# Decoder layer in split float32: the order of the products inside a weight slot pair, bank by bank or product by product

## The chip, the cores and the metric

One core of a Trainium2 chip runs one launch of the kernel. The metric is device time in microseconds (us). Before the change the median of three runs is 2539.82 us, the lowest 2538.85 and the highest 2540.03.

## The reference, cut to what matters

The reference is one step (one layer) of a hybrid decoder on 256 prompt tokens and 8 x 4 sample tokens, 288 in all, with width 2048:

```python
x = x + 0.5 * _swiglu(_rmsnorm(x, g_ffn1), w1_gate, w1_up, w1_down)   # 2048 -> 5504 -> 2048
h = _rmsnorm(x, g_mix)
proj = h @ w_in                                                        # 2048 -> 7192
...        # forgetting attention on 8 heads, mLSTM on 8 heads, causal convolution, gates
x = x + y @ w_out                                                      # 2048 -> 2048
x = x + 0.5 * _swiglu(_rmsnorm(x, g_ffn2), w2_gate, w2_up, w2_down)
# _swiglu(x, g, u, d) = (silu(x @ g) * (x @ u)) @ d
```

All is float32, and the answer has to be near float32 accuracy. The time lies in the eight big products with a weight matrix (gate, up and down twice, w_in, w_out); all weights are read from HBM once.

## The kernel before, in words

**Split operands.** A float32 matrix is cut into two parts that TensorE multiplies in its faster rounded type: `hi`, the value rounded, and `lo`, what is left. A product w * x is the sum of three: w_hi * x_hi, w_hi * x_lo and w_lo * x_hi. The activations stand transposed, one tile of 128 rows by T = 288 tokens for each of the 16 (or 24, or 19) blocks of the contraction, and they are the moving operand. A 128 x 128 block of the weights is the stationary operand, loaded anew for each matmul.

**Slots, turns and pairs.** The weights come in pieces of 128 x 1024 float32 (512 KB), one per block of the contraction, into `w_raw`, which has four slots. SyncE issues the transfers. ScalarE rounds a slot into `w_hi` (L544), VectorE subtracts to make `w_lo` (L766). Four slots are a turn. TensorE works through a turn in two pairs of slots; it waits for both `w_lo` of the pair, and its last matmul of the pair raises `w_used`, which lets ScalarE overwrite the pair.

**Groups and banks.** A group is an output of up to 8 blocks of 128 columns, accumulated in the 8 banks of PSUM over 4 turns (contraction 2048), 6 turns (3072) or 5 turns (19 blocks, so that the last pair holds one slot). The groups in order, with their number: `gu0a` 6, `down0a` 2, `gu0b` 4, `gu0c` 1 (with 6 banks), `down0b` 2 (19 blocks), then the mixer `in_a` 3, `in_m` 4 and `out` 2, then `gu1a` to `down1b` as in the first SwiGLU. In a gate and up group (`gu...`) the even banks hold gate blocks, the odd ones up blocks.

**Order inside a pair.** The function `turn_products` goes bank by bank: for a bank, for each slot of the pair, the three products (L1257, L1258, L1259), so 6 matmuls in a row write one bank before the next bank has its 6. That makes 48 matmuls a pair.

**Handing over the banks.** There is one set of 8 banks, so a group writes where the one before it wrote. In the last pair of a group each bank is closed after its 6 matmuls (`bank_done`, or `w_used` for the last bank), and the bank is read while TensorE closes the others. In a gate and up group ScalarE takes SiLU of an even bank (L598) and VectorE multiplies with the odd bank (L839); a multiply frees its two banks, and the last multiply frees all that are left (banks 4 to 7 in `gu0c` and `gu1c`). In a down group VectorE adds each bank to the residual `X` (L867), in `in_a` and `in_m` it copies it out (L918, L1112 and L1113, L1117). Each raises `banks_free`. In its first pair the next group waits for `banks_free` ahead of its first matmul into each bank.

**Order of the other engines.** Each has one list written by hand, in loops. VectorE prepares the first two slots of the next group (L766) and then empties the banks.

Of the kernel before, what the change touches and what calls it, by code (L numbers as in the profile page):

```python
# [37 lines left out]
P = 128  # L38
# [6 lines left out]
T = TP + SM  # L45
# [14 lines left out]
SLOTS = 4  # L60
NBANK = 8
# [32 lines left out]
def build(nc, A, O):  # L94
# [48 lines left out]
    w_hi, w_lo = t_("w_hi", [P, SLOTS, UW], F32R), t_("w_lo", [P, SLOTS, UW], F32R)  # L143
# [6 lines left out]
    ps = ctx.enter_context(nc.psum_tensor("ps", [P, NBANK, 512], F32))  # L150
# [103 lines left out]
    w_hi_ready, w_lo_ready, w_used = sem("w_hi_ready"), sem("w_lo_ready"), sem("w_used")  # L254
    bank_done, banks_free = sem("bank_done"), sem("banks_free")
# [986 lines left out]
    def _(pe):  # L1242
        mm, tr = nc.tensor.matmul, nc.tensor.transpose

        def turn_products(g, turn0, gi, kt, x_hi, x_lo, first, last, x_ready):

            for pair in range(2):
                slots = [s for s in (2 * pair, 2 * pair + 1) if not (last and 0 < g.real % SLOTS <= s)]
                pe.wait_ge(w_lo_ready, (turn0 + kt) * SLOTS + (2 * pair + 2))
                pe.wait_ge(x_ready[0], kt * SLOTS + (x_ready[1] + slots[-1] + 1))  # L1250
                for b, c in enumerate(g.tiles):
                    if first and pair == 0:
                        pe.wait_ge(banks_free, gi * NBANK + (b + 1))
                    out = ps[:, b, 0:T]
                    for s in slots:
                        hi, lo, k = w_hi[:, s, c:c + P], w_lo[:, s, c:c + P], kt * SLOTS + s
                        mm(out, hi, x_hi[:, k, :], start=first and pair == 0 and s == slots[0], stop=False)  # L1257
                        mm(out, hi, x_lo[:, k, :], start=False, stop=False)  # L1258
                        ins = mm(out, lo, x_hi[:, k, :], start=False, stop=last and pair == 1 and s == slots[-1])  # L1259
                    if b == len(g.tiles) - 1:  # L1260
                        ins.then_inc(w_used, 1)
                    elif last and pair == 1:
                        ins.then_inc(bank_done, 1 if b < len(g.tiles) - 2 else NBANK + 1 - len(g.tiles))

        def group_products(g, i, x_hi, x_lo, x_ready):

# [56 lines left out]
        for t in range(KD):  # L1323
            if t >= 4:
                pe.wait_ge(sem("xT_copied"), t - 3)
            for r, n in TT:
                ins = tr(ps[:, 1 + t % 4, r * P:r * P + n], x_rows[0:n, r, t * P:(t + 1) * P], ident[0:n, 0:n])
# [18 lines left out]
        for k in range(KD):  # L1346
# [3 lines left out]
            ins = mm(gates, w_gates_lo[:, k, :], xm_hi[:, k, :], start=False, stop=k == KD - 1)  # L1350
# [3 lines left out]
        for t, n in TT:  # L1354
            ins = tr(ps[0:n, 3, t * 3 * H:(t + 1) * 3 * H], gates_row[:, t * P:t * P + n], ident[0:3 * H, 0:3 * H])
# [94 lines left out]
        for h in range(H):  # L1450
            ins = mm(bhq(ps[0:SM, 7, 0:256])[:, :, h, :], ka[:, h, TP:T], qa[:, h, TP:T], start=True, stop=True)
# [12 lines left out]
        for g2 in range(2):  # L1464
# [6 lines left out]
            ins = mm(o2, spread[:, r], mask4_q[:, :], **add)  # L1471
        ins.then_inc(sem("sample_logits"), 1)
        for g2 in range(2):
# [3 lines left out]
            ins = tr(ps[0:SM, 1, g2 * P:(g2 + 1) * P], Ps[:, g2, 2 * P:T], ident[:, :])  # L1477
# [6 lines left out]
        for p in range(NB * NPG):  # L1484
            pe.wait_ge(sem(f"v_loaded{p % VRING}"), 16 * (p // VRING + 1))
            pe.wait_ge(sem("pz_ready"), p + 1)
            for h in range(H):
                ins = mm(ps[0:SM, 2 + h // 4, h % 4 * HD:(h % 4 + 1) * HD], pz[:, p % 4, h * SM:(h + 1) * SM],  # L1488
                         v_page[p % VRING][:, h * HD:(h + 1) * HD], **add)
            ins.then_inc(sem("sample_pv"), 1)  # L1490
        for h in range(H):
            pe.wait_ge(sem("out_rows_ready"), 1 + h // 4)
            ins = tr(ps[:, 1, h * SM:(h + 1) * SM], out_rows[:, h * HD:(h + 1) * HD], ident[0:SM, 0:SM])
# [19 lines left out]
        for j in range(2 * H):  # L1513
            ins = tr(ps[:, 5, j * 24:(j + 1) * 24], conv_rows[0:24, j * P:(j + 1) * P], ident[0:24, 0:24])
# [8 lines left out]
        for b in range(2):  # L1523
            for j in range(4):
                ins = mm(ps[:, 6 + b, j * 96:(j + 1) * 96], sel[:, 4 * b + j, :].bitcast(F32), s_rows[:, :, :], start=True, stop=True)
# [136 lines left out]
```

## Time and profile before

| | |
|---|---|
| median of 3 runs | 2539.82 us |
| span of the profiled execution, first to last instruction | 2540.0 us |
| TensorE busy, matmuls | 2423.9 us, 95%, 17636 records |
| TensorE weight loads | 2348.2 us, 92% |
| VectorE busy | 1197.0 us, 47% |
| ScalarE busy | 905.7 us, 36% |
| mean granted TensorE clock | 0.971 |
| DMA | 151 GB/s mean, 46.8% of the queues' time on the main one |

The profile page gives no other time for that execution than its span. It lies 0.2 us above the median of the runs, so terms read from the trace can be added to the median as they are. Matmuls overlap one another: one that lasts 0.29 us starts 0.13 us after the one before it, so a pace is read from starts, not from durations. A time such as 105.92 is counted from the start of the span.

### The profile page before, as it was taken

The page shows a single profiled execution, that of the slowest core. Times are in us where ns is not written, and L with a number is a line of the kernel's source. Part 1 is how long each engine was busy: PE and PEld are TensorE (multiplying, and loading weights), DVE is VectorE, ACT ScalarE, POOL GpSimd, SP SyncE. Part 2 cuts the span into 40 slices and gives each one's busy share as a digit, 9 for nine tenths or more (in the row PEclk, how much of TensorE's full clock was granted, in tenths as well). Part 3 has the DMA queues.
Part 4 walks back from the last instruction along what each step waited for, and adds up shares of the span by engine and source line. Part 5 has one row for each costly group of instructions (what it writes and reads, how often), then busy time and mean ns, then how long its engine had stood idle before and what let it go on. Part 6 is the DMA issues. An engine that isn't in the chain of part 4 may idle for free.

```text
span 2540.0 us, 47708 instructions
## 1 busy us (share of the span) xinstructions
PE 2423.9 (95%) x17636; PEld 2348.2 (92%) x17636; DVE 1197.0 (47%) x1664; ACT 905.7 (36%) x1139; POOL 83.7 (3%) x96
## 2 busy tenths in 40 slices
PE   5999999999999989898899897989999999999997
PEld 4999999999999989778899875979999999999997
DVE  5444544344454464543347665454444444444543
ACT  3444433333343433321234323344444333333432
POOL 1000000000000000000000241000000000000000
PEclk9999999999999999989999887989999999999998
DMA  3555555555555535434255441435555444555553
GB/s 108 166 165 165 165 166 165 164 166 165 166 167 166 166 117 165 159 102 158 89 165 165 130 115 39 166 108 158 165 165 166 164 164 162 167 165 162 169 172 127
DMA packets 172981, 383.79 MB, mean 151 GB/s; under 512 B 18629, under 2 KB 44333, under 8 KB 172285
## 3 DMA queue, kind: packets, MB, share of 16 engines
q1 hardware_dynamic: 170144, 374.94, 46.8%
q0 software_dynamic: 2432, 5.57, 0.7%
q10 hardware_dynamic: 336, 2.36, 0.2%
q8 instruction: 44, 0.72, 0.1%
q14 instruction: 25, 0.20, 0.0%
HBM read 373.09 MB, written 9.70 MB: 151 GB/s over the span
## 4 chain that ended last, share of the span: by engine, by line
PE 91%; DVE 6%; ACT 1%; issue 1%; DMA 1%; POOL 0%; SPq 0%; ACTq 0%; DVEq 0%; POOLq 0%
PE ps L1259 27%; PE ps L1257 27%; PE ps L1258 27%; PE ps L1431 1%; PE ps L1283 1%; PE ps L1488 1%; DVE xt L811 1%; PE ps L1594 1%; DMA w_raw<-in_w_up 1%; PE ps L1585 1%; DVE w_lo L766 1%; PE ps L1292 1%; PE ps L1299 1%; PE ps L1418 1%; DVE x_lo L801 0%
## 5 line engine op out<-in xcount | busy, mean ns | idle before, releaser
L766 DVE TENSOR_TENSOR w_lo<-w_raw,w_hi 128x1024 fp32r<-128x1024 f32 x674 | 795.6, 1222 | 1109.8 <-ACT w_hi L544 1109.8
L544 ACT CAST w_hi<-w_raw 128x1024 fp32r<-128x1024 f32 x674 | 673.9, 1047 | 1294.5 <-PE ps L1259 1279.9
L1257 PE MATMUL ps<-x_hi,w_hi 128*128 128x288 f32 (+1 forms) x2752 | 817.6, 297 | 19.2 <-DVE x_lo L801 14.7
L1259 PE MATMUL ps<-x_hi,w_lo 128*128 128x288 f32 (+1 forms) x2752 | 819.3, 298 | 0.0
L1258 PE MATMUL ps<-x_lo,w_hi 128*128 128x288 f32 (+1 forms) x2752 | 805.9, 293 | 0.0
L1257 PEld LDWEIGHTS ps<-x_hi,w_hi 128*128 128x128 f32 x2752 | 520.4, 189 | 20.2 <-issue 20.2
L1258 PEld LDWEIGHTS ps<-x_lo,w_hi 128*128 128x128 f32 x2752 | 528.4, 192 | 0.0
L1259 PEld LDWEIGHTS ps<-x_hi,w_lo 128*128 128x128 f32 x2752 | 518.8, 189 | 0.0
L1257 PE MATMUL ps<-hid_hi,w_hi 128*128 (+1 forms) x1376 | 407.6, 296 | 1.5 <-DVE X L867 1.5
L1258 PE MATMUL ps<-hid_lo,w_hi 128*128 (+1 forms) x1376 | 406.2, 295 | 0.0
L1259 PE MATMUL ps<-hid_hi,w_lo 128*128 (+1 forms) x1376 | 405.0, 294 | 0.0
L1257 PE MATMUL ps<-xm_hi,w_hi 128*128 128x288 f32 (+1 forms) x896 | 267.5, 299 | 12.2 <-DVE xm_lo L801 7.1
L1259 PE MATMUL ps<-xm_hi,w_lo 128*128 128x288 f32 (+1 forms) x896 | 267.6, 299 | 0.0
L1258 PE MATMUL ps<-xm_lo,w_hi 128*128 128x288 f32 (+1 forms) x896 | 263.4, 294 | 0.0
L1257 PEld LDWEIGHTS ps<-hid_hi,w_hi 128*128 128x128 f32 x1376 | 258.1, 188 | 1.9 <-DVE X L867 1.9
L1259 PEld LDWEIGHTS ps<-hid_hi,w_lo 128*128 128x128 f32 x1376 | 259.4, 188 | 0.0
L1258 PEld LDWEIGHTS ps<-hid_lo,w_hi 128*128 128x128 f32 x1376 | 258.4, 188 | 0.0
L1257 PEld LDWEIGHTS ps<-xm_hi,w_hi 128*128 128x128 f32 x896 | 170.4, 190 | 13.0 <-issue 13.0
L1258 PEld LDWEIGHTS ps<-xm_lo,w_hi 128*128 128x128 f32 x896 | 173.1, 193 | 0.0
L1259 PEld LDWEIGHTS ps<-xm_hi,w_lo 128*128 128x128 f32 x896 | 169.8, 190 | 0.0
L1257 PE MATMUL ps<-y_hi,w_hi 128*128 128x288 f32 (+1 forms) x256 | 76.8, 300 | 1.4 <-DVE y_lo L801 1.4
L1259 PE MATMUL ps<-y_hi,w_lo 128*128 128x288 f32 (+1 forms) x256 | 76.8, 300 | 0.0
(405 smaller groups left out, 1595.7 us busy)
## 6 DMA issues: line engine op xcount, KB each, us to landing
w_raw<-in_w_down SPq DMA_DIRECT2D x178, 512.0 KB
w_raw<-in_w_gate SPq DMA_DIRECT2D x320, 256.0 KB
w_raw<-in_w_up SPq DMA_DIRECT2D x320, 256.0 KB
w_raw<-in_w_in SPq DMA_DIRECT2D x112, 512.0 KB
w_raw<-in_w_out SPq DMA_DIRECT2D x32, 512.0 KB
page<-in_cache_k SPq DMA_DIRECT2D x16, 512.0 KB, 3.4
w_raw<-in_w_gate SPq DMA_DIRECT2D x32, 192.0 KB
w_raw<-in_w_up SPq DMA_DIRECT2D x32, 192.0 KB
```

The source lines that it names most:

```text
L544: nc.scalar.copy(w_hi[:, slot, :], w_raw[:, slot, :]).then_inc(w_hi_ready, 1)
L766: nc.vector.tensor_tensor(w_lo[:, slot, :], w_raw[:, slot, :], w_hi[:, slot, :].bitcast(F32), ALU.subtract).then_inc(w_lo_ready, 1)
L811: nc.vector.scalar_tensor_tensor(xt[:, t % 2, :], X[:, t, :], vecs[:, gain + t:gain + t + 1], rs[:, 1, :], ALU.mult, ALU.mult).then_inc(se ...
L1257: mm(out, hi, x_hi[:, k, :], start=first and pair == 0 and s == slots[0], stop=False)
L1258: mm(out, hi, x_lo[:, k, :], start=False, stop=False)
L1259: ins = mm(out, lo, x_hi[:, k, :], start=False, stop=last and pair == 1 and s == slots[-1])
L1283: mm(ps[:, bank, 0:T], ones[:, :], sq_ring[i % 4], start=stop_start[0], stop=stop_start[1]).then_inc(sem("sum_done"), 1)
L1292: mm(out, sel[:, h, :], parts[0], start=start, stop=False)
L1299: mm(ps[0:H, bank + j // H, 0:T], one_hot[:, j % H, :], sq_ring[(i0 + j) % 4], start=j % H == 0, stop=j % H == H - 1).then_inc(sem("sum_do ...
L1418: ins = tr(ps[:, 5 + 2 * half, i * P:(i + 1) * P], page[:, p % 3, c:c + HD], ident[:, :])
L1431: ins = mm(ps[r:r + SM, 6, col:col + P], qz[:, b % 2, h * SM:(h + 1) * SM], kpT[:, p % 2, h * HD:(h + 1) * HD], start=b < 4 and c == 0 and ...
L1488: ins = mm(ps[0:SM, 2 + h // 4, h % 4 * HD:(h % 4 + 1) * HD], pz[:, p % 4, h * SM:(h + 1) * SM], v_page[p % VRING][:, h * HD:(h + 1) * HD] ...
```

## The change: products outside, banks inside

In every pair but the last of a group, the loops are turned round: for each slot of the pair, for each of the three products, all eight banks (six in `gu0c` and `gu1c`). So eight matmuls in a row share the moving operand and go to eight banks. The last pair of a group keeps the old order, since the banks are closed there one after another. Number, shapes and operands of the matmuls are the same. `w_used` is raised by the last matmul of a pair, as before. The wait for each bank in a group's first pair stands ahead of the first matmul into that bank, as before. No other engine's list changes. All three products now stand on one line (L1257).

```diff
-                for b, c in enumerate(g.tiles):
-                    if first and pair == 0:
-                        pe.wait_ge(banks_free, gi * NBANK + (b + 1))
-                    out = ps[:, b, 0:T]
+                n, ending = len(g.tiles), last and pair == 1
+
+                def product(out, s, c, part, start, stop):
+
+                    k = kt * SLOTS + s
+                    w, x = ((w_hi, x_hi), (w_hi, x_lo), (w_lo, x_hi))[part]
+                    return mm(out, w[:, s, c:c + P], x[:, k, :], start=start, stop=stop)
+
+                if ending:
+                    for b, c in enumerate(g.tiles):
+                        for s in slots:
+                            for part in range(3):
+                                ins = product(ps[:, b, 0:T], s, c, part, False, s == slots[-1] and part == 2)
+                        if b == n - 1:
+                            ins.then_inc(w_used, 1)
+                        else:
+                            ins.then_inc(bank_done, 1 if b < n - 2 else NBANK + 1 - n)
+                else:
                     for s in slots:
-                        hi, lo, k = w_hi[:, s, c:c + P], w_lo[:, s, c:c + P], kt * SLOTS + s
-                        mm(out, hi, x_hi[:, k, :], start=first and pair == 0 and s == slots[0], stop=False)
-                        mm(out, hi, x_lo[:, k, :], start=False, stop=False)
-                        ins = mm(out, lo, x_hi[:, k, :], start=False, stop=last and pair == 1 and s == slots[-1])
-                    if b == len(g.tiles) - 1:
-                        ins.then_inc(w_used, 1)
-                    elif last and pair == 1:
-                        ins.then_inc(bank_done, 1 if b < len(g.tiles) - 2 else NBANK + 1 - len(g.tiles))
+                        for part in range(3):
+                            for b, c in enumerate(g.tiles):
+                                opening = first and pair == 0 and s == slots[0] and part == 0
+                                if opening:
+                                    pe.wait_ge(banks_free, gi * NBANK + (b + 1))
+                                ins = product(ps[:, b, 0:T], s, c, part, opening, False)
+                    ins.then_inc(w_used, 1)
```

The opening pair of a group, on TensorE, before (`x_hi` and `x_lo` are the moving operand; `REGISTER_ALU` sets the number that the next wait compares with):

```order
L1253 ISA [waits xn_ready,w_lo_ready]
L1257 MATMUL ps<-x_hi,w_hi 128x288 [waits banks_free]
L1258 MATMUL ps<-x_lo,w_hi 128x288
L1259 MATMUL ps<-x_hi,w_lo 128x288
L1257 MATMUL ps<-x_hi,w_hi 128x288
L1258 MATMUL ps<-x_lo,w_hi 128x288
L1259 MATMUL ps<-x_hi,w_lo 128x288
L1253 REGISTER_ALU
L1257 MATMUL ps<-x_hi,w_hi 128x288 [waits banks_free]
```

The same pair on TensorE in the changed kernel, from the seventh bank's wait on; six such matmuls with a wait, one per bank, stand ahead of it:

```order
L1257 MATMUL ps<-x_hi,w_hi 128x288 [waits banks_free]
L1274 REGISTER_ALU
L1257 MATMUL ps<-x_hi,w_hi 128x288 [waits banks_free]
L1257 MATMUL ps<-x_lo,w_hi 128x288 x8
L1257 MATMUL ps<-x_hi,w_lo 128x288 x8
L1257 MATMUL ps<-x_hi,w_hi 128x288 x8
L1257 MATMUL ps<-x_lo,w_hi 128x288 x8
L1257 MATMUL ps<-x_hi,w_lo 128x288 x8
L1249 REGISTER_ALU
```

The eight waits for a bank stood ahead of the 1st, 7th, 13th ... 43rd matmul of the group; they now stand ahead of the 1st, 2nd, 3rd ... 8th.

Inside the loop over the middle turns, one pair on TensorE before, its first matmuls:

```order
L1250 ISA [waits w_lo_ready]
L1257 ISA [waits xn_ready]
L1257 MATMUL ps<-x_hi,w_hi 128x288
L1258 REGISTER_ALU
L1258 MATMUL ps<-x_lo,w_hi 128x288
L1259 MATMUL ps<-x_hi,w_lo 128x288
```

The same pair in the changed kernel, whole:

```order
L1250 ISA [waits w_lo_ready]
L1257 ISA [waits xn_ready]
L1257 MATMUL ps<-x_hi,w_hi 128x288 x8
L1257 REGISTER_ALU
L1257 MATMUL ps<-x_lo,w_hi 128x288 x8
L1257 MATMUL ps<-x_hi,w_lo 128x288 x8
L1257 ISA
L1257 MATMUL ps<-x_hi,w_hi 128x288 x8
L1257 REGISTER_ALU
L1257 MATMUL ps<-x_lo,w_hi 128x288 x8
L1257 MATMUL ps<-x_hi,w_lo 128x288 x8
```

The waits and the register instructions of such a pair are the same, in front of the same products; what moved is only the order of its 48 matmuls.

## Rows read from the trace of the kernel before

**Rows 1.** The page: busy times; TensorE's busy tenths and granted clock in 40 slices.
```profile
PE 2423.9 (95%) x17636; PEld 2348.2 (92%) x17636; DVE 1197.0 (47%) x1664; ACT 905.7 (36%) x1139; POOL 83.7 (3%) x96
PE   5999999999999989898899897989999999999997
PEclk9999999999999999989999887989999999999998
```
**Rows 2.** The page's groups: line, operation, tiles, count | busy us, mean ns | idle before.
```profile
L1257 PE MATMUL ps<-x_hi,w_hi 128*128 128x288 f32 (+1 forms) x2752 | 817.6, 297 | 19.2 <-DVE x_lo L801 14.7
L1257 PE MATMUL ps<-hid_hi,w_hi 128*128 (+1 forms) x1376 | 407.6, 296 | 1.5 <-DVE X L867 1.5
L1257 PE MATMUL ps<-xm_hi,w_hi 128*128 128x288 f32 (+1 forms) x896 | 267.5, 299 | 12.2 <-DVE xm_lo L801 7.1
L1257 PE MATMUL ps<-y_hi,w_hi 128*128 128x288 f32 (+1 forms) x256 | 76.8, 300 | 1.4 <-DVE y_lo L801 1.4
```
**Rows 3.** Timeline, TensorE: first matmul of four groups. Start us, duration us, what.
```profile
105.92 0.30 PE L1257 MATMUL ps<-x_hi,w_hi 128*128 128x288 f32 x1
...
156.70 0.30 PE L1257 MATMUL ps<-x_hi,w_hi 128*128 128x288 f32 x1
...
359.79 0.30 PE L1257 MATMUL ps<-hid_hi,w_hi 128*128 128x288 f32 x1
...
436.58 0.30 PE L1257 MATMUL ps<-hid_hi,w_hi 128*128 128x288 f32 x1
```
**Rows 4.** Timeline, TensorE: the matmuls from one bank to the next.
```profile
106.46 0.29 PE L1258 MATMUL ps<-x_lo,w_hi 128*128 128x288 f32 x1
106.59 0.30 PE L1259 MATMUL ps<-x_hi,w_lo 128*128 128x288 f32 x1
106.73 0.29 PE L1257 MATMUL ps<-x_hi,w_hi 128*128 128x288 f32 x1
```
**Rows 5.** Timeline, TensorE: the gates, 24 weight columns; 14 rows between these left out.
```profile
1052.79 0.29 PE L1349 MATMUL ps<-xm_lo,w_gates_hi 128*24 128x288 f32 x1
...
1054.77 0.29 PE L1349 MATMUL ps<-xm_lo,w_gates_hi 128*24 128x288 f32 x1
```
**Rows 6.** Timeline, TensorE, at a granted clock of 0.50; 5 rows between left out.
```profile
67.09 0.44 PE L1257 MATMUL ps<-x_hi,w_hi 128*128 x1
...
68.53 0.44 PE L1257 MATMUL ps<-x_hi,w_hi 128*128 x1
```
**Rows 7.** Timeline, VectorE, where the down group at 816.22 follows another.
```profile
813.44 2.36 DVE L766 TENSOR_TENSOR w_lo<-w_raw,w_hi 128x1024 fp32r<-128x1024 f32 x2 [4.04 <-ACT w_hi L544]
815.71 3.00 DVE L867 SCALAR_TENSOR_TENSOR X<-ps,X 128x288 f32<-128x288 f32 x8
```
**Rows 8.** Timeline, TensorE, the same place.
```profile
815.18 0.29 PE L1259 MATMUL ps<-hid_hi,w_lo 128*128 128x288 f32 x1
816.22 0.40 PE L1257 MATMUL ps<-hid_hi,w_hi 128*128 128x288 f32 x1 [0.74 <-DVE X L867]
816.45 0.29 PE L1258 MATMUL ps<-hid_lo,w_hi 128*128 128x288 f32 x1
816.58 0.29 PE L1259 MATMUL ps<-hid_hi,w_lo 128*128 128x288 f32 x1
```
**Rows 9.** Timeline: first matmul after `gu0c`, and the last multiply of `gu0c`.
```profile
754.56 0.30 PE L1257 MATMUL ps<-hid_hi,w_hi 128*128 128x288 f32 x1
...
754.86 0.45 DVE L839 TENSOR_TENSOR prod<-silu,ps 128x288 f32<-128x288 f32 x1 [0.63 <-PE ps L1259]
```
**Rows 10.** Timeline: last reading of the banks at three group starts, and the third start.
```profile
106.20 0.46 DVE L839 TENSOR_TENSOR prod<-silu,ps 128x288 f32<-128x288 f32 x1 [1.13 <-PE ps L1259]
436.78 0.46 DVE L867 SCALAR_TENSOR_TENSOR X<-ps,X 128x288 f32<-128x288 f32 x1 [0.34 <-PE ps L1259]
...
1278.02 0.30 PE L1257 MATMUL ps<-xm_hi,w_hi 128*128 128x288 f32 x1
...
1278.57 0.18 DVE L1113 COPY ext<-ps 128x32 f32<-128x32 f32 x1
```
**Rows 11.** Windows: us, busy us (count) by engine, granted clock, DMA share, GB/s.
```profile
62.90:66.20 3.30, 0.87 (x7) 0.64 (x5) 2.59 (x3) 3.30 (x4) 0.00 (x0) 1.00 0.07 7
66.20:69.60 3.40, 3.38 (x14) 3.39 (x15) 2.04 (x2) 1.35 (x2) 0.00 (x0) 0.50 0.89 262
69.60:73.00 3.40, 3.40 (x27) 3.40 (x26) 0.00 (x0) 0.14 (x1) 0.00 (x0) 0.99 0.96 318
815.00:818.50 3.50, 2.76 (x21) 2.53 (x20) 3.50 (x9) 2.00 (x2) 0.00 (x0) 1.00 0.67 176
```

## The prediction

> **What bounds the kernel now.** I read the busy times first: TensorE is busy 95% of 2540.0 us and its clock is at full in nearly every slice, while VectorE and ScalarE are about half idle [rows 1]. Then the groups: the products of the big matrices are 3 x (2752 + 896 + 256) = 11,712 matmuls with `x`, `xm` or `y` as moving operand and 3 x 1376 = 4128 with `hid`, and before them TensorE idled only 19.2 + 1.5 + 12.2 + 1.4 us in all [rows 2]. Then the starts in the timeline. A group with `x` takes 156.70 - 105.92 = 50.78 us for 384 matmuls, 0.1322 us each; one with `hid` takes 436.58 - 359.79 = 76.79 us for 576, 0.1333 us each [rows 3]. That makes 11,712 x 0.1322 + 4128 x 0.1333 = 2099 us of the span. So two things can move the time: the pace of these matmuls, and what TensorE waits for between groups.
>
> **How many matmuls move.** The last pair of each group keeps its order: 29 groups of 48 and two of 36 matmuls on the `x` side (1464), four of 48 and four of 24 on the `hid` side (288). The rest, 10,248 + 3840 = 14,088, come in the new order.
>
> **The pace (taken at no change).** The number, shape and operands of the matmuls stay. Three things in their neighbourhood change: the bank written is another each time, the moving operand stays for eight, and the stationary operand is never the one just loaded.
> - The bank. Inside a bank the step is 0.13, the step onto the next bank is 0.14, at a reading of 0.01 [rows 4]. Writing one bank six times over costs nothing that a new bank saves.
> - The weight load. The gates' matmuls load 24 columns in place of 128 and go at (1054.77 - 1052.79) / 15 = 0.132 [rows 5]. The load is not what sets the pace.
> - The moving operand. At half the clock 288 columns take (68.53 - 67.09) / 6 = 0.24 [rows 6], so at full clock 0.12 would do, and 0.012 to 0.013 of each matmul is something else. It is larger for `hid` than for `x` with the same weights and instructions [rows 3], so it goes with the operand that streams. Each operand streams as often as before.
> No row has two matmuls in a row with one moving tile. So the bounds are wide: down to 0.12 if the extra goes away, which is 10,248 x 0.0122 + 3840 x 0.0133 = -176 us, and up to 0.14, the longest step read, which is 10,248 x 0.0078 + 3840 x 0.0067 = +106 us. I take 0, since the two parts that I can vary in the rows do nothing.
>
> **The waits for the banks.** Here something is lost. Bank 7 was needed 42 matmuls after a group's start, 42 x 0.132 = 5.5 us; it is now needed after 7, 0.93 us. VectorE frees the banks at the pace that it has. The one place where TensorE already waits for a bank gives the price of a wait: VectorE's first addition ends at 815.71 + 0.45 = 816.16 (0.45 for one, as in [rows 10]), the matmul starts at 816.22, 0.06 later, and the next only 0.23 after it instead of 0.13 [rows 7, 8]. A stall so costs the wait, 0.06 and 0.10 for the restart. There are 34 group starts with no norm or attention ahead of them, of four kinds.
> - `down0b` and `down1b`, second group, 2 starts. The last pair of the group before has one slot, so TensorE closes its banks in half the time, and VectorE first makes `w_lo` (till 815.7), then frees eight banks in 3.00 us, one each (3.00 - 0.45) / 7 = 0.364, the last at 818.71 [rows 7]. Before, TensorE had six matmuls (0.8 us) for each bank and waited once. Now it takes one matmul each time a bank comes free, the eighth at 818.77, the ninth at 819.00. Before, the ninth started at 816.45 + 7 x 0.133 = 817.38. That is 1.62 us, twice: **3.2 us**.
> - The start after `gu0c` and `gu1c`, 2 starts. Banks 4 to 7 are freed by one multiply that ends at 754.86 + 0.45 = 755.31; the fifth matmul starts at 755.37, the sixth at 755.60, instead of 754.56 + 5 x 0.133 = 755.23 [rows 9]. 0.37 us, twice: **0.7 us**.
> - The start after another gate and up group, 20 starts. Banks 6 and 7 are freed at 106.20 + 0.46 = 106.66 [rows 10]; the seventh matmul is due at 105.92 + 6 x 0.132 = 106.71 and its weight load one step earlier. So the wait lands on the load: matmul at 106.72, the eighth at 106.95 instead of 106.85. 0.10 us each: **2.0 us**. Bounds: 0, if the load still fits behind the matmul before it, and 0.2, if the whole restart step comes on top.
> - The other 10 starts. After `down`, `in_a` and `out` groups the last bank is free at 436.78 + 0.46 = 437.24, and the eighth matmul is due at 436.58 + 0.93 = 437.51. In `in_m` it is free at 1278.57 + 0.18 = 1278.75 and due at 1278.02 + 0.93 = 1278.95 [rows 10]. Nothing, at the price above; cover 0.2 to 0.3 us.
> What is delayed on TensorE is not made up later, for its other waits on these lines are the 34 us above, nearly all at norms, which start from TensorE's own last matmul. The weights lie ready: at 813.44 VectorE had idled 4.04 us for ScalarE's rounding, which waits for TensorE to release a slot [rows 7], and that release comes at the end of a pair as before.
>
> The sum: 3.2 + 0.7 + 2.0 + 0 = 5.9 us on a span of 2540.0. The span is within 0.2 us of the median, so 2539.8 + 5.9 = **2545.7 us**, 0.23% more.
>
> **The clock.** At 816 to 819 TensorE will have eight matmuls in some 3.5 us. The row for that is 62.90 to 66.20: 7 matmuls at full clock, and in the stretch behind it the granted clock is 0.50 and 14 matmuls were started, against 27 in the next at full [rows 11]. Such a fall costs (27 - 14) x 0.13 = 1.7 us. But 815.00 to 818.50, with a gap of 1.04 us in it and 21 matmuls, kept its clock [rows 11]. So between none and 3.4 us for the two places; I leave it out of the sum and keep it in the range.
> The Trainium skill has a rule that speaks against this change, in "TensorE: Matmul & The Clock Gate", section "A second HAM failure mode: psum-queue depth-cycling": a kernel that cycled through its PSUM banks each iteration had small idle times between its groups of matmuls, and TensorE's clock went down and up again and again. By that rule each start with a wait, 24 of them, could lose its clock; the trace agrees only in part, since the one such start that it has, with 1.04 us idle, stayed at full clock. That is the rival "clock" below.
> The same skill, in "Perfetto Trace Analysis", section "Matmuls", wants independent groups to rotate through the banks so that the emptying of one overlaps the next group's matmuls. The order before does this at a group's start; the new one gives it 0.93 us of the 5.5.
>
> **The rivals.**
> - Waits hidden (not slower). TensorE runs the weight load of bank 6 behind the matmul before it, so that the 20 starts cost nothing, and a bank's restart costs less at the two `down` starts, where the next wait covers it. 3.2 + 0.7 = 3.9 us or a little less: 2543.7, within 0.2%. For it: the margin at the 20 starts is only a few hundredths of a us, which is the reading of the trace.
> - Pace slower. `x` gets the pace of `hid`, as its streams now come eight from one tile: 10,248 x 0.0011 = 11.3 us more, 2557. Against: nothing in the rows ties the pace to what came before.
> - Pace faster. If a step with the same weights loaded again is one of the longer steps and every step becomes 0.130, 10,248 x 0.0022 + 3840 x 0.0033 = 35 us less, 2511. If the extra goes with changing the moving tile and falls off for seven of eight, 7/8 of 176, 154 us less: 2392. For it: the 0.012 has no cause that I can show. Against: steps of 0.13 and 0.14 mix at random inside a bank and across banks.
> - Clock. A fall at each of 24 starts: 24 x 1.7 = 41 us, 2587.
> - That the order does not change on the engine: excluded, since the instruction list shows it.
>
> **How the numbers follow.** No change that a measurement of this kernel can tell is within 0.2%, 5.1 us: 2534.7 to 2544.9. Forecast (5 to 9 us more, with or without one fall of the clock): 0.45. Waits hidden: 0.26. Pace slower: 0.11. Clock: 0.02. Pace faster, a little: 0.11, much: 0.05. Faster 0.16; same 0.26, and 0.01 from the forecast's lower edge, 0.27; slower the rest, 0.57. The range takes in the forecast, the hidden waits and the slower pace: 2540 to 2558, which leaves out the faster cases and the clock, 0.18. The likeliest case by itself is 2544 to 2550.
>
> **What would show each step.** Right: starts inside the moved pairs still 0.132 apart for `x` and 0.133 for `hid` (384 matmuls of a group in 50.8 to 50.9 us); in the group at 816, eight matmuls 0.36 apart and the ninth near 819.0; idle time of TensorE on this line put down to VectorE's L867 and L839, 4 to 6 us more than before; the second and later starts of a gate and up group with one step of about 0.23 at the seventh or eighth matmul. Wrong: a pace that differs by 0.001 or more moves the time by 14 us and outweighs all the waits. A granted clock of 0.50 behind 819 or 2460 would show the fall.

## The result, and the profile after

| | before | after |
|---|---|---|
| median, us (lowest to highest, runs) | 2540.03 (2538.85 to 2544.42, 7) | 2550.54 (2546.40 to 2553.76, 7) |
| profiled execution: span, us | 2540.0 | 2550.5 |

The changed kernel takes 1.0037 times as long, with a 95% interval of 1.0026 to 1.0047: 6.6 to 11.9 us more. The two medians differ by 10.5 us, the two means by 9.4. The forecast was 5.9 us more, 2545.7; the median lies 4.8 us above it, inside the range, and 0.5 us above what was called the likeliest case, 2544 to 2550. The mean granted clock of the profiled execution of after is 0.969. The device time is 1.6 to 1.8 us above the span in every run that has both. The profiled execution of before has a span of 2540.0 and no device time on record; by that difference it was one of about 2541.6 and not the median one.

The page of after, its busy times, TensorE's slices and two groups [rows 1, 2]:

```profile
PE 2433.8 (95%) x17636; PEld 2352.3 (92%) x17636; DVE 1197.2 (47%) x1664; ACT 906.4 (36%) x1139; POOL 83.7 (3%) x96
...
PE   5999999999999989898899897989999999999997
...
PEclk9999999999999999989999887989999999999999
...
L1257 PE MATMUL ps<-x_hi,w_hi 128*128 128x288 f32 (+1 forms) x2752 | 476.6, 298 | 19.2 <-DVE x_lo L801 14.7
...
L1257 PE MATMUL ps<-hid_hi,w_hi 128*128 (+1 forms) x1376 | 228.1, 296 | 1.7 <-DVE X L867 1.5
```

Nothing stands out. The busy time of the first group was 817.6 us before; it is lower only because eight matmuls of the group now follow and overlap one another, and the mean of one, 298 ns for 297, has not changed. TensorE's idle time before these matmuls has hardly grown, since a matmul held back for 0.1 or 0.2 us still overlaps the one before it in the records. The busy share of the page can't show this change; TensorE is busy for 9.9 us more, doing the same.

What TensorE's weight load waited for, from the waits of after (us in total, times, longest):

```profile
PEld ps L1257 <- DVE X L867: 4.4, 16, 1.0
...
PEld ps L1257 <- DVE prod L839: 0.7, 2, 0.3
```

The first row was 1.9 us in 2 waits before, the second was not there. Sixteen waits are the eight banks of the two `down` starts. Of what TensorE waits for on these lines nothing else grows by more than a us. The prediction wanted 4 to 6 us more idle time put down to L867 and L839. These rows have 3.2 us, all of it before weight loads; the matmuls' own row, 1.5 us for L867, is the same before and after. The waits have to be read from the starts.

The starts. TensorE at the group that stood at 816.22 before [rows 8], in the timeline of after:

```profile
817.68 2.95 PE L1257 MATMUL ps<-hid_hi,w_hi 128*128 128x288 f32 x8 [0.75 <-DVE X L867]
...
820.47 0.56 PE L1257 MATMUL ps<-hid_lo,w_hi 128*128 128x288 f32 x3
```

and VectorE there [rows 7]:

```profile
814.90 2.36 DVE L766 TENSOR_TENSOR w_lo<-w_raw,w_hi 128x1024 fp32r<-128x1024 f32 x2 [4.00 <-ACT w_hi L544]
817.17 3.00 DVE L867 SCALAR_TENSOR_TENSOR X<-ps,X 128x288 f32<-128x288 f32 x8
```

VectorE does what it did before, eight banks in 3.00 us, and TensorE takes eight matmuls for it, the ninth 2.79 us after the first. Before, the ninth came 1.16 us after it (0.237 and seven steps of 0.13). The seven steps are 0.364 each and the last 0.237.

TensorE at the two group starts that stood at 105.92 and 156.70, and behind the first of them, in the timeline of after [rows 3]:

```profile
106.14 1.31 PE L1257 MATMUL ps<-x_hi,w_hi 128*128 128x288 f32 x8
107.29 1.22 PE L1257 MATMUL ps<-x_lo,w_hi 128*128 128x288 f32 x8
...
157.13 0.30 PE L1257 MATMUL ps<-x_hi,w_hi 128*128 128x288 f32 x1
```

Eight matmuls in 107.29 - 106.14 = 1.15 us, where eight steps of 0.132 are 1.06: one step, onto the eighth bank, is 0.218. The group takes 157.13 - 106.14 = 50.99 us for 50.78 before.

The start of `gu0c`, which has six banks, follows a gate and up group too, but there nothing is lost. Six matmuls take 718.63 - 717.83 = 0.80 us, six steps of 0.133:

```profile
717.83 0.96 PE L1257 MATMUL ps<-x_hi,w_hi 128*128 128x288 f32 x6
718.63 0.95 PE L1257 MATMUL ps<-x_lo,w_hi 128*128 128x288 f32 x6
```

The start behind `gu0c` [rows 9], its fourth matmul, its fifth and its ninth (rows of three windows, so that their counts overlap):

```profile
756.39 0.81 PE L1257 MATMUL ps<-hid_hi,w_hi 128*128 128x288 f32 x2
...
756.80 0.79 PE L1257 MATMUL ps<-hid_hi,w_hi 128*128 128x288 f32 x4
757.43 0.82 PE L1257 MATMUL ps<-hid_lo,w_hi 128*128 128x288 f32 x5
```

The fifth comes 0.41 us after the fourth, and the four from it on take 0.63 us, where four steps of 0.132 are 0.53.

And the granted clock. Three stretches with norms, attention or the mLSTM in them, cut at the same instructions in both kernels to within a matmul; before (window: us, busy us and count of PE, PEld, DVE, ACT and POOL, granted clock, DMA share, GB/s):

```profile
876.20:894.92 18.72, 9.03 (x40) 6.82 (x40) 12.88 (x23) 11.63 (x23) 5.90 (x11) 0.93 0.39 116
999.58:1224.68 225.10, 198.17 (x1432) 171.99 (x1431) 98.16 (x219) 58.33 (x121) 5.40 (x9) 0.92 0.40 130
1379.56:1567.02 187.46, 164.12 (x943) 130.54 (x941) 129.35 (x216) 59.98 (x121) 55.52 (x41) 0.85 0.34 102
```

and after:

```profile
878.95:899.24 20.29, 10.60 (x41) 7.83 (x40) 12.89 (x23) 11.67 (x23) 6.69 (x13) 0.84 0.36 107
1004.11:1231.76 227.65, 202.47 (x1432) 174.87 (x1431) 98.36 (x219) 58.58 (x121) 5.40 (x9) 0.90 0.38 129
1387.10:1574.31 187.21, 163.93 (x942) 130.38 (x941) 129.44 (x216) 60.01 (x121) 55.52 (x41) 0.85 0.34 101
```

VectorE and ScalarE do the same work in the same busy time, and TensorE has the same number of matmuls, one more or less at the cuts. In the first two stretches the granted clock is lower in after and the stretch is longer; in the third both are about the same. Over the three that is 1.57 + 2.55 - 0.25 = 3.9 us. With 5.6 us of waits and 0.9 us of pace (both below) that makes 10.4 of the 10.5 us between the two spans.

### The profile page after: what moved, and what is told of

The parts are those of the page before. It is cut to its first block, busy times and chain, and to the rows that moved or that the text cites. A ratio compares the mean times of both kernels' runs of the same rounds, so it can differ in the third digit from the quotient of the medians.

```text
span 2550.5 us, 47708 instructions
## 1 busy us (share of the span) xinstructions
PE 2433.8 (95%) x17636; PEld 2352.3 (92%) x17636; DVE 1197.2 (47%) x1664; ACT 906.4 (36%) x1139; POOL 83.7 (3%) x96
## 4 chain that ended last, share of the span: by engine, by line
PE 92%; DVE 5%; ACT 1%; issue 1%; DMA 1%; POOL 0%; SPq 0%; ACTq 0%; DVEq 0%; POOLq 0%
PE ps L1257 81%; PE ps L1296 1%; PE ps L1444 1%; PE ps L1501 1%; DVE xt L811 1%; PE ps L1607 1%; DMA w_raw<-in_w_up 1%; PE ps L1598 1%; PE ps L1431 1%; PE ps L1305 1%; DVE w_lo L766 1%; PE ps L1312 1%; DVE x_lo L801 0%; PE ps L1379 0%; ACT w_hi L544 0%
## 5 line engine op out<-in xcount | busy, mean ns | idle before, releaser
L1257 PE MATMUL ps<-x_hi,w_hi 128*128 128x288 f32 (+1 forms) x2752 | 476.6, 298 | 19.2 <-DVE x_lo L801 14.7
L1257 PE MATMUL ps<-x_lo,w_hi 128*128 128x288 f32 (+1 forms) x2752 | 472.6, 296 | 0.0
L1257 PE MATMUL ps<-x_hi,w_lo 128*128 128x288 f32 (+1 forms) x2752 | 471.5, 295 | 0.0
L1257 PEld LDWEIGHTS ps<-x_hi,w_hi 128*128 128x128 f32 x2752 | 404.8, 190 | 21.0 <-issue 20.2
L1257 PEld LDWEIGHTS ps<-x_lo,w_hi 128*128 128x128 f32 x2752 | 405.1, 190 | 0.0
L1257 PEld LDWEIGHTS ps<-x_hi,w_lo 128*128 128x128 f32 x2752 | 401.1, 189 | 0.0
L1257 PE MATMUL ps<-hid_hi,w_hi 128*128 (+1 forms) x1376 | 228.1, 296 | 1.7 <-DVE X L867 1.5
L1257 PE MATMUL ps<-hid_lo,w_hi 128*128 (+1 forms) x1376 | 223.8, 294 | 0.0
L1257 PE MATMUL ps<-hid_hi,w_lo 128*128 (+1 forms) x1376 | 223.8, 294 | 0.0
L1257 PEld LDWEIGHTS ps<-hid_hi,w_hi 128*128 128x128 f32 x1376 | 197.3, 188 | 5.3 <-DVE X L867 4.4
L1257 PEld LDWEIGHTS ps<-hid_hi,w_lo 128*128 128x128 f32 x1376 | 196.5, 188 | 0.0
L1257 PEld LDWEIGHTS ps<-hid_lo,w_hi 128*128 128x128 f32 x1376 | 196.5, 188 | 0.0
L1257 PE MATMUL ps<-xm_hi,w_hi 128*128 128x288 f32 (+1 forms) x896 | 155.5, 299 | 12.4 <-DVE xm_lo L801 7.1
L1257 PE MATMUL ps<-xm_lo,w_hi 128*128 128x288 f32 (+1 forms) x896 | 154.1, 297 | 0.0
L1257 PE MATMUL ps<-xm_hi,w_lo 128*128 128x288 f32 (+1 forms) x896 | 153.7, 296 | 0.0
L1257 PEld LDWEIGHTS ps<-xm_hi,w_hi 128*128 128x128 f32 x896 | 132.3, 191 | 13.2 <-issue 13.2
L1257 PEld LDWEIGHTS ps<-xm_lo,w_hi 128*128 128x128 f32 x896 | 132.3, 191 | 0.0
L1257 PEld LDWEIGHTS ps<-xm_hi,w_lo 128*128 128x128 f32 x896 | 131.1, 190 | 0.0
L839 DVE TENSOR_TENSOR prod<-silu,ps 128x288 f32<-128x288 f32 x86 | 37.0, 451 | 35.9 <-PE ps L1257 35.1
```

Source lines behind the costliest of these rows:

```text
L839: nc.vector.tensor_tensor(prod[:, j, :], silu[:, j, :], ps[:, 2 * j + 1, 0:T], ALU.mult).then_inc(banks_free, freed)
L1257: return mm(out, w[:, s, c:c + P], x[:, k, :], start=start, stop=stop)
```

## The experiments

Eight kernels, with runs of the kernel before beside them. All of them have the pair written as one list of (bank, slot, product), with the place of the pair in its group as a condition. The orders, brought together from their kernels, with two comments added (below, a line with `rule` is cut to the rule of that kernel):

```diff
+                if rule == "bank":        # the order before
+                    todo = [(b, s, part) for b in range(n) for s in slots for part in range(3)]
+                elif rule == "product":   # the changed order
+                    todo = [(b, s, part) for s in slots for part in range(3) for b in range(n)]
+                elif rule == "slot":
+                    todo = [(b, s, part) for s in slots for b in range(n) for part in range(3)]
+                elif rule == "diagonal":
+                    six = [(s, part) for s in slots for part in range(3)]
+                    todo = [(b, *six[(b + r) % len(six)]) for r in range(len(six)) for b in range(n)]
+                elif rule == "two":
+                    todo = [(b, s, part) for b0 in range(0, n, 2) for s in slots for part in range(3) for b in (b0, b0 + 1)]
```

A pair is `opening` (the first of a group, with the waits for the banks), `ending` (the last, bank by bank in all kernels) or `middle`. The matmuls of all of them stand on one line, L1275 in most. "Step" below is the time from one matmul's start to the next. Its mean is taken from one trace of each kernel, over the middle pairs of the 26 `x` groups of eight banks and the eight `hid` groups that ran at the full granted clock throughout. In the kernel before it is 132.22 ns for `x` and 133.33 ns for `hid`, after 132.62 and 132.50. The expectations have 132.23 and 132.65 for `x`, a less exact reading.

### Without the waits

```diff
-                rule = "bank" if place == "ending" else "product"    # the changed kernel, in this form
+                rule = "product" if place == "middle" else "bank"
```

> The opening pair of each group goes back to bank by bank; the middle pairs stay product by product. Theory (waits): the 24 starts lose their stall, which the trace of the changed kernel shows as 20 x 0.085 + 2 x 0.38 + 2 x 1.62 = 5.7 us, and what is left against the kernel before is the pace alone: 0.4 ns more for each moved x matmul, 0.8 ns less for each moved hid matmul, together within 1 us; the second down0b group shows one step of 0.24 and none of 0.36. So 2540 to 2542 us, same as before. Rival (order): the slowdown lies in the order of the middle pairs and the stages behind them, and 2 us or more of the 10 stay beyond the waits: 2544 or more.

Measured: 2541.27 us (2538.89 to 2548.10, 12 runs) with before beside it at 2542.38 (21 runs), ratio to before 1.0001 [0.9988, 1.0013]. TensorE at the start that took eight matmuls in 2.79 us, and a window of this kernel that is one of the three above:

```profile
815.18 0.40 PE L1275 MATMUL ps<-hid_hi,w_hi 128*128 128x288 f32 x1 [0.74 <-DVE X L867]
815.42 0.29 PE L1275 MATMUL ps<-hid_lo,w_hi 128*128 128x288 f32 x1
```

```profile
1000.13:1227.64 227.51, 202.66 (x1432) 174.88 (x1431) 98.30 (x219) 58.58 (x121) 5.40 (x9) 0.90 0.38 129
```

The start is as it was before: one restart step of 0.24, then 0.13. A gate and up group takes 50.89 us. With only the opening pair put back the loss is gone, so it sits in the opening pairs, where the waits for the banks are, and not in the other 87% of the reordered matmuls. This is what the theory of the waits expected; the rival wanted 2544 or more. (The 20 starts in the expectation are 18, see below.) The window says one thing more: this kernel has no new wait, and its attention stretch was as long, at a granted clock of 0.90, as that of after. A longer stretch of that kind so does not need the waits.

### The waits alone

```diff
+                rule = "product" if place == "opening" else "bank"
```

> Only the opening pair of each group is product by product, the middle pairs are bank by bank as before. Theory (waits): 5.7 us more than before, 2545 to 2547 us, with the same steps of 0.217, 0.408 and 0.364 at the group starts as in the changed kernel, and a pace of 0.1322 (x) and 0.1333 (hid) in the middle. Rival (order): under 3 us more than before.

Measured: 2549.13 us (2546.09 to 2551.59, 10 runs) with before beside it at 2542.38, ratio 1.0029 [1.0019, 1.0040]. TensorE at the same two kinds of start:

```profile
817.94 2.95 PE L1275 MATMUL ps<-hid_hi,w_hi 128*128 128x288 f32 x8 [0.75 <-DVE X L867]
```

```profile
106.36 0.82 PE L1275 MATMUL ps<-x_hi,w_hi 128*128 128x288 f32 x5
107.01 0.66 PE L1275 MATMUL ps<-x_hi,w_hi 128*128 128x288 f32 x3
107.51 1.21 PE L1275 MATMUL ps<-x_lo,w_hi 128*128 128x288 f32 x8
```

Both are as in after, and 107.51 - 106.36 = 1.15 us again; over the 18 starts of this kind the long step is 0.216 to 0.235 us. The opening pairs alone, 1848 of the 14,088 reordered matmuls, bring most of the loss. The time is above the expected 2545 to 2547, which counted from 2540; against before in the same session it is 6.8 us more, for 5.7 expected. The rival, under 3 us, is out. Together with the kernel before this one it gives the cost of the waits without any change of pace elsewhere.

### What sets the pace: same bank, other order of the products

```diff
+                products = {"hl": ((w_hi, x_hi), (w_hi, x_lo), (w_lo, x_hi)),
+                            "hh": ((w_hi, x_hi), (w_lo, x_hi), (w_hi, x_lo))}
+                rule, form = "bank", ("hh" if place == "middle" else "hl")
```

> Bank by bank everywhere, as before; in the middle pairs the three products stand as w_hi x_hi, w_lo x_hi, w_hi x_lo, so that the moving operand is repeated in one step of three and no stationary operand is loaded twice in a row. Theory (moving operand): a third of the way to the changed kernel or more, hid group 76.4 to 76.7 us, x group 50.8 to 50.9. Rival (stationary operand not repeated): the whole way, 76.35 and 50.90. Rival (bank): as before, 76.80 and 50.77.

One run: 2539.17 us. TensorE at two starts of `x` groups and at the second `down` start with the group behind it:

```profile
103.76 0.29 PE L1275 MATMUL ps<-x_hi,w_hi 128*128 128x288 f32 x1
...
154.53 0.29 PE L1275 MATMUL ps<-x_hi,w_hi 128*128 128x288 f32 x1
...
434.42 0.30 PE L1275 MATMUL ps<-hid_hi,w_hi 128*128 128x288 f32 x1
...
511.21 0.29 PE L1275 MATMUL ps<-x_hi,w_hi 128*128 128x288 f32 x1
```

50.77 and 76.79 us, as before to the hundredth; steps 132.22 and 133.33 ns. No weight tile is loaded twice in a row here and the moving operand stays for two matmuls, and neither moves the pace: the theory of the moving operand and the rival of the weight tile missed, and the rival "bank" came out as it stands.

### What sets the pace: another bank each time

```diff
+                rule = "diagonal" if place == "middle" else "bank"
```

> Middle pairs alone in a third order: the bank changes at each matmul, but the moving operand follows hi, lo, hi, hi, lo, hi as before (bank b takes product number b + round of the six), and no stationary operand is loaded twice in a row. Read from the length of the groups. Theory (moving operand): pace as before, 50.77 us for an x group and 76.8 us for a down0a group. Rival (bank, or a stationary operand not repeated): pace as in the changed kernel, 0.4 ns more for x (50.90 us a group) and 0.8 ns less for hid (76.35 us).

One run: 2542.93 us.

```profile
103.96 0.29 PE L1275 MATMUL ps<-x_hi,w_hi 128*128 128x288 f32 x1
...
154.85 0.29 PE L1275 MATMUL ps<-x_hi,w_hi 128*128 128x288 f32 x1
...
435.01 0.30 PE L1275 MATMUL ps<-hid_hi,w_hi 128*128 128x288 f32 x1
...
511.61 0.29 PE L1275 MATMUL ps<-x_hi,w_hi 128*128 128x288 f32 x1
```

50.89 and 76.60 us; steps 132.64 and 132.93 ns. With the bank changed at each matmul, and the moving tile held only from one round of eight to the next (5 times in 48), `x` has the pace of after and `hid` half of its gain: the theory missed, its rival came out for `x` and by half for `hid`. So how the banks are walked does move the pace.

### Two more walks through the banks

```diff
+                rule = "slot" if place == "middle" else "bank"     # one kernel
+                rule = "two" if place == "middle" else "bank"      # the other
```

> Middle pairs: slot outside, then bank, then the three products, so that the bank changes at every third matmul instead of every sixth. Theory (each change of bank has its own small price): before has 8 changes in 48 and 132.23, the kernels with 48 changes in 48 have 132.65; with 16 changes x goes to 132.23 + 0.42 x 8/40 = 132.3, hid from 133.33 to about 133.2. Rival (threshold, nothing happens until every matmul changes the bank): 132.23 and 133.33.

> Middle pairs: two banks take turns at each matmul (the six products of banks 0 and 1, then of 2 and 3, ...), so a matmul never follows one into its own bank but comes back to it after one. Theory (it matters only whether the matmul before wrote the same bank): the pace of the changed kernel, 132.6 for x and about 132.5 for hid. Rival (it matters how long ago the bank was written): a pace between before and the changed kernel, x nearer to 132.2 and hid nearer to 133.3.

One run each: 2543.00 us for "slot", 2547.08 us for "two". TensorE in "slot":

```profile
103.60 0.30 PE L1275 MATMUL ps<-x_hi,w_hi 128*128 128x288 f32 x1
...
154.49 0.30 PE L1275 MATMUL ps<-x_hi,w_hi 128*128 128x288 f32 x1
...
434.43 0.30 PE L1275 MATMUL ps<-hid_hi,w_hi 128*128 128x288 f32 x1
...
510.82 0.29 PE L1275 MATMUL ps<-x_hi,w_hi 128*128 128x288 f32 x1
```

and in "two":

```profile
106.72 0.29 PE L1277 MATMUL ps<-x_hi,w_hi 128*128 128x288 f32 x1
...
157.57 0.29 PE L1277 MATMUL ps<-x_hi,w_hi 128*128 128x288 f32 x1
...
437.51 0.30 PE L1277 MATMUL ps<-hid_hi,w_hi 128*128 128x288 f32 x1
...
514.04 0.29 PE L1277 MATMUL ps<-x_hi,w_hi 128*128 128x288 f32 x1
```

| middle pairs | changes of bank in 48 matmuls | changes of slot | step `x`, ns | step `hid`, ns |
|---|---|---|---|---|
| bank by bank (before) | 7 | 15 | 132.22 | 133.33 |
| two banks in turn | 47 | 7 | 132.49 | 132.79 |
| slot, bank, product | 15 | 1 | 132.63 | 132.51 |
| product by product (after) | 47 | 1 | 132.62 | 132.50 |
| diagonal | 47 | 14 | 132.64 | 132.93 |

"slot" keeps the three products of one bank together, as before, and changes the bank only at each third matmul; it has the pace of after on both sides. So it is not a new bank at each matmul that counts, nor eight matmuls with one moving tile. Both expectations for "slot" missed, a small shift and none at all; for "two" the steps came out about two thirds of the way from before to after, between the theory and its rival. In the first four rows fewer changes of slot go with a faster `hid` and a slower `x`, but the diagonal does not fit into that for `x`. Why `x` loses what `hid` gains stays open. What the traces show, one for each kernel, is the size: never more than 0.8 ns of 133 in either direction.

### A version with the gain alone

Since only `hid` gets faster and the opening pairs bring only waits, two kernels take the middle pairs of the `down` groups and nothing else. Alone:

```diff
+                rule = "product" if place == "middle" and down else "bank"
```

> Product by product only where it made matmuls faster: the middle pairs of the down groups (hid). All x groups, all opening and ending pairs as before. Theory (the bank that a matmul follows sets a small part of its pace, in a way that differs by operand): 480 moved matmuls in a down0a group save 0.8 ns each, 0.40 us, 384 in a down0b group 0.32 us, in all 2.9 us; x groups 50.77 us as before; 2537 where before has 2540, ratio 0.9989. Rival: the gain is eaten by the stages behind, ratio 1.000 with the same group lengths.

Measured: 2539.75 us (2534.63 to 2542.44, 11 runs), before beside it 2542.22 (22 runs), ratio 0.9988 [0.9977, 0.9999].

```profile
106.18 0.29 PE L1275 MATMUL ps<-x_hi,w_hi 128*128 128x288 f32 x1
...
156.95 0.29 PE L1275 MATMUL ps<-x_hi,w_hi 128*128 128x288 f32 x1
...
436.44 0.30 PE L1275 MATMUL ps<-hid_hi,w_hi 128*128 128x288 f32 x1
...
512.84 0.29 PE L1275 MATMUL ps<-x_hi,w_hi 128*128 128x288 f32 x1
```

50.77 us for the `x` group, as before, and 76.40 for `hid`, 0.4 less. The middle pairs of the `down` groups are 3456 matmuls, and 3456 x 0.82 ns = 2.8 us is what the step promises; 0.0012 of 2542 is 3.1 us. The theory came out, in the lengths and in the time.

And with VectorE freeing bank 0 of the first `down0b` and `down1b` group before it makes `w_lo`, so that the group at 816.22 need not wait for both (`early` is 1 in these two groups and 0 in the other `down` groups):

```diff
                 for half in range(2):
-                    split_turns(half * g.turns + g.turn, g.turns)
-                    residual(g, half, 0.5)
+                    split_turns(half * g.turns + g.turn, g.turns, pair=False)
+                    if half == 0:
+                        residual(g, half, 0.5, range(early))
+                    split_pair((half + 1) * g.turns + g.turn, 0)
+                    residual(g, half, 0.5, range(early if half == 0 else 0, NBANK))
```

> As the kernel with only the down groups product by product, and in addition VectorE empties bank 0 of the first down0b and down1b group before it makes w_lo of the next group's first two slots. Before, TensorE started 0.4 us after that w_lo, held by bank 0. Theory: the second group starts 0.35 us earlier, twice 0.35 = 0.7 us on top of 2.9: 3.6 us less than before, ratio 0.9986. Rival: w_lo is made later by as much, since VectorE waits for the bank, and nothing is gained over the kernel without it.

Measured: 2538.29 us (2532.77 to 2542.89, 12 runs), ratio 0.9987 [0.9976, 0.9998]. VectorE and TensorE at that start:

```profile
810.71 2.36 DVE L766 TENSOR_TENSOR w_lo<-w_raw,w_hi 128x1024 fp32r<-128x1024 f32 x2 [0.23 <-ACT w_hi L544]
812.99 2.64 DVE L872 SCALAR_TENSOR_TENSOR X<-ps,X 128x288 f32<-128x288 f32 x7
```

```profile
752.16 0.30 PE L1280 MATMUL ps<-hid_hi,w_hi 128*128 128x288 f32 x1
...
813.22 0.39 PE L1280 MATMUL ps<-hid_hi,w_hi 128*128 128x288 f32 x1 [0.47 <-DVE w_lo L766]
```

Seven banks are left behind `w_lo`, not eight, and the wait of TensorE is 0.47 us, now for `w_lo`, where it was 0.74. The group ahead takes 813.22 - 752.16 = 61.06 us, 0.28 less than in the kernel without this edit (61.34), twice: 0.6 us for the 0.7 expected, which its timing can't tell from that of its neighbour. This kernel has the lowest median of all here, about 0.1% below before, and is not told apart from the one without the edit.

### The same runs at the same clock

Each run comes with its mean granted clock (the seven first runs of before have none on record). The other 95 runs of the six timed kernels, 43 of them before, were fitted with parallel lines: 1.7 us less for each 0.001 more, +-0.4. In the 43 runs of before the clock goes from 0.968 (2546.8 us, mean of 3) to 0.973 (2537.9, mean of 9). The distance to before at the same clock, from a fit with one slope and a level for each kernel (+- is two standard errors), beside what the traces give:

| | at the same clock, us | from the trace, us |
|---|---|---|
| after | +7.5 +- 1.8 | waits 5.6, pace 0.9 |
| opening pairs alone | +6.0 +- 1.5 | waits 5.7 |
| middle pairs alone | +1.6 +- 1.5 | pace 0.7 |
| middle pairs of `down` alone | -2.7 +- 1.5 | pace -2.8 |
| the same, bank 0 early | -3.3 +- 1.4 | pace -2.8, start -0.6 |

All five agree. What is left of the 10.5 us between the two spans goes with the clock. The runs of after and of the opening pairs alone have a mean clock of 0.9701 and 0.9702, the other four 0.9708 to 0.9716. With a spread of 0.0013 from run to run and 7 and 10 runs each is at the edge of what can be told. Taken together, the 17 runs with the new waits lie 0.0008 below the 78 others, a bit more than two standard errors, which at 1.7 us for each 0.001 is 1.3 us. Against it stand the ten traces, one for each kernel. The attention stretch takes 227.1 to 227.7 us in six of them, of which four have no new wait (middle pairs alone, two banks, "slot", bank 0 early), and 224.9 to 226.3 us in the other four. The three stretches together take 435.2 us in after, 429.0 to 435.9 in the others, and 431.3 in the opening pairs alone, as in before. So a long stretch doesn't need the waits, and whether they lower the clock a little stays open.

## Why the prediction was right, point by point

- **Waits for the banks, 5.9 us forecast.** Right. The two `down` starts: seven steps of 0.364 and one of 0.237, against 0.237 and seven of 0.133, is 1.62 us each, 3.2 as forecast. After `gu0c` and `gu1c` the steps onto the fifth and sixth bank are 0.408 and 0.238, 0.38 each; forecast 0.37. The starts behind another gate and up group were counted as 20, and 18 of them lose something. The other two are the starts of `gu0c` and `gu1c`, which have six banks and so never come to the late ones. The 18 have one step of 0.216 to 0.225 for 0.132, 0.085 to 0.09 each, 1.6 us; forecast 0.10 and 2.0 us. In the trace of after the last multiply ends at 106.41 + 0.45 = 106.86 and the seventh matmul starts at 106.94, 0.08 later and on time; the loss shows on the eighth. In the trace with the opening pairs alone that step is 0.216 to 0.235, 0.229 in the mean, which makes 1.7 us of the 1.6. The ten other starts lost nothing, but for one step of 0.147 in one of them. Sum 5.6 us. The price for a stall, the wait and 0.06 for the release and about 0.10 for the restart [rows 7, 8], so held at the three kinds of start. At the 18 starts of both traces the seventh matmul comes 0.06 to 0.08 us behind the end of the multiply and the eighth 0.29 to 0.30, which is 0.06 and a step of 0.237: the earlier the multiply ends before the seventh matmul, the shorter the long step (0.077 and 0.217 us, 0.062 and 0.235).
- **Pace, 0 forecast.** The step that failed, though its error is small in the sum: `x` 0.40 ns slower, 10,248 x 0.40 = +4.1 us, `hid` 0.83 ns faster, 3840 x 0.83 = -3.2 us, together +0.9. The argument "writing one bank six times over costs nothing that a new bank saves" rested on steps of 0.13 and 0.14 us read at 0.01 [rows 4], and the effect is 0.0004 to 0.0008 us; only a length over hundreds of matmuls, as in [rows 3], can show it. Of the three arguments two hold in the order of the kernel before, as far as they were tried: a weight tile loaded again doesn't move the pace, and a repeated moving tile doesn't. The third, that the bank doesn't, falls with the diagonal and "slot", as far as bank and slot can be told apart at all. That the sum came out near 0 was luck of the counts.
- **The rivals.** "Waits hidden" is refuted: 18 of its 20 starts pay, and the two `down` starts cost 3.2 us and no less. "Pace slower" had the direction right for `x`, where the shift is a good third of the forecast one (0.40 ns for 1.1), and missed that `hid` would move the other way. "Pace faster" would have needed -2.2 ns. "Clock", a fall at each start with a wait: refuted at its best place. The window behind the stall of after at 817.68 has 13 matmuls in 3.5 us:

```profile
817.50:821.00 3.50, 3.32 (x13) 2.08 (x14) 3.50 (x9) 1.46 (x2) 0.00 (x0) 1.00 0.80 274
```

  and its granted clock is 1.00. So it is over the whole of the two stretches of after that hold all 22 starts with a loss:

```profile
72.00:880.00 808.00, 807.11 (x6067) 804.72 (x6065) 356.43 (x411) 302.48 (x323) 0.00 (x0) 1.00 0.51 164
1720.00:2525.00 805.00, 804.14 (x6046) 801.97 (x6045) 354.41 (x409) 300.52 (x321) 0.00 (x0) 1.00 0.50 164
```

  The rule of the Trainium skill that the prediction weighed ("TensorE: Matmul & The Clock Gate", section "A second HAM failure mode: psum-queue depth-cycling") so does not reach waits of this size in this kernel.
- **The own time of the profiled execution.** I set its span beside the median of the runs and called them 0.2 us apart. A span has to have 1.6 us added before it is compared; that the two nearly agreed was chance. The sum doesn't suffer from it, since it adds a difference to a median of device times. But that median came from three runs: the 43 later runs of before have medians of 2542.38 and 2542.22, so the base was low by some 2 us.
- **What was missing** is the clock in the stages with norms and attention. I looked for a fall of the clock where the change makes TensorE wait, and not where the clock falls anyway and where the length of the fall differs from run to run: 3.9 us between these two traces. The runs of before alone go from 2535.95 to 2549.36 us, and the clock of these two runs, 0.973 and 0.969, accounts for 7 of the 13 us by the fit. That 2550.54 lay inside the range is owed in part to its width, which was meant for the slower pace.

## What to carry to other kernels

Turning a loop so that all PSUM banks are opened within one round of matmuls takes from each bank the time that the others gave it: compare the time at which each bank is needed in the new order with the time at which the reader lets it go, start by start, and price each late one at the wait, 0.06 us and a 0.10 us restart. Look also at how many banks a group really opens. The inner pairs open nothing, and five orders of them differed by 0.8 ns a matmul at most, so change them alone and leave the opening and the closing pair as they are. A pace that differs by half a nanosecond comes to microseconds over thousands of matmuls, and is read only from the length of a whole group; two kernels that differ by 0.1% are compared at the same mean clock.

## What the runs showed of the hardware

- The step of a 128x288 matmul in this number format depends on the order in which weight tiles, slots and banks are walked, by up to 0.8 ns of 133, and in opposite directions for two moving operands of the same shape (`x` 132.22 to 132.62, `hid` 133.33 to 132.50 ns). No rule that fits all five orders was found.
- In a chain of waits on VectorE, each followed by one matmul, TensorE's steps were 0.362 to 0.366 us, VectorE's own pace of 0.364 us a bank; the restart of 0.10 us shows only once, at the end (0.237 for 0.133).
- Banks that came free 0.06 to 0.08 us before the seventh matmul was due still cost one long step behind it, 0.216 to 0.235 us for 0.132, at 18 starts in each of two traces. The eighth matmul came 0.29 to 0.30 us after VectorE's instruction ended in all 36 cases.
- Eight matmuls spread over 2.8 us, in a window with 13 in 3.5 us, left the granted clock at 1.00, there and in the 808 and 805 us around the 22 starts with a loss.
- The mean granted clock of runs of one kernel lay between 0.968 and 0.973, worth about 9 us of 2540.
